# Two transformer blocks on one core: remainder splits, norms and gating rows moved in the order, projection b reads a buffer of its own, down projections start a hidden pair early

## The reference, cut to what matters

```python
# first block
gate_a = sigmoid(...); gate_b = sigmoid(...)
ya = s5_branch(...)                      # [256, 512]
yb = gelu(zu) * (w_s @ layer_norm(gelu(zv)) + bias)   # spatial gating, [256, 1024]
merged = gate_a * (ya @ w_proj_a) + gate_b * (yb @ w_proj_b)
h = h + merged @ w_out
h = h + memory_cross_attention(rms_norm(h, g), memn, ...)
h = h + (silu(hn @ w_gate) * (hn @ w_up)) @ w_down    # F = 2816
# second block, passes c0, x0, c1, x1 (context/tokens of layer 0, 1)
...  merged = sum(gate_i * (y_i @ w_i)) ; h = h + merged @ w_out
...  h = h + (silu(hn @ w1) * (hn @ w3)) @ w2
```

## Time and profile before

| | us |
|---|---|
| median of 3 runs | 2396.34 |
| lowest, highest | 2386.43, 2405.35 |
| the profiled execution, its own time | 2400.58 |
| its span | 2398.1 |
| PE busy | 2208.5 |
| DVE busy | 1619.3 |
| ACT busy | 1006.9 |
| mean granted TensorE clock (share, not us) | 0.964 |

### The profile page before, as it was taken

How to read it: one execution, slowest core, us unless ns; L and a number is a source line. 1 busy time by engine, 2 the same in 40 slices (tenths; PEclk the granted TensorE clock), 3 DMA queues, 4 the chain that set the end, 5 groups by cost and what they waited for, 6 DMA issues and landing times.

```text
span 2398.1 us, 42021 instructions
## 1 busy us (share of the span) xinstructions
PE 2208.5 (92%) x17181; PEld 2064.1 (86%) x17181; DVE 1619.3 (68%) x2081; ACT 1006.9 (42%) x1189; POOL 206.4 (9%) x201
## 2 busy tenths in 40 slices
PE   8898898899999889999999779999999977999998
PEld 6676887799999878899999668899999966889998
DVE  8987554656588876665578967665557896766554
ACT  4114335543444454443444355444344435444332
POOL 3761002100000110000000110000000011000000
PEclk9999999999999999999999889999999988999999
DMA  7678564565555333455555223456545432234552
GB/s 245 245 279 319 208 243 136 177 204 176 188 176 159 123 106 124 158 185 185 179 175 163 88 71 105 142 158 200 186 151 175 141 106 71 89 123 153 180 184 79
DMA packets 290478, 392.99 MB, mean 164 GB/s; under 512 B 8518, under 2 KB 256669, under 8 KB 283677
## 3 DMA queue, kind: packets, MB, share of 16 engines
q1 hardware_dynamic: 285620, 383.53, 49.4%
q10 hardware_dynamic: 3624, 6.31, 0.8%
q0 software_dynamic: 1088, 1.10, 0.2%
HBM read 387.66 MB, written 3.15 MB: 163 GB/s over the span
## 4 chain that ended last, share of the span: by engine, by line
PE 74%; DVE 15%; ACT 4%; issue 3%; DMA 2%; POOL 1%; DVEq 0%; SPq 0%; ACTq 0%
PE L L847 59%; PE M L847 3%; DVE w_rest L430 3%; PE L L1101 2%; PE M L984 2%; PE L L1087 1%; DVE m L1963 1%; DVE n_rest L1972 1%; ACT w_high L424 1%; DMA raw<-in_w_in 1%; PE M L1334 1%; DVE work L2465 1%; DVE work L2593 1%; PE L L1114 1%; DVE rstd L1960 1%
## 5 line engine op out<-in xcount | busy, mean ns | idle before, releaser
L847 PE MATMUL L<-n_high,w_high 128*128 128x256 f32 x3424 | 982.4, 287 | 40.6 <-DVE w_rest L430 20.4
L847 PE MATMUL L<-n_rest,w_high 128*128 128x256 f32 x3424 | 966.2, 282 | 0.0
L847 PE MATMUL L<-n_high,w_rest 128*128 128x256 f32 x3424 | 966.0, 282 | 0.0
L430 DVE TENSOR_TENSOR w_rest<-raw,w_high 128x2048 fp32r<-128x2048 f32 x293 | 671.0, 2292 | 251.3 <-PE L L847 244.0
L424 ACT ACTIVATE w_high<-raw 128x2048 fp32r<-128x2048 f32 x293 | 560.9, 1915 | 398.4 <-PE L L847 364.8
L847 PEld LDWEIGHTS L<-n_high,w_high 128*128 128x128 f32 x3424 | 660.2, 193 | 63.0 <-issue 40.2
L847 PEld LDWEIGHTS L<-n_rest,w_high 128*128 128x128 f32 x3424 | 659.0, 192 | 0.6
L847 PEld LDWEIGHTS L<-n_high,w_rest 128*128 128x128 f32 x3424 | 658.6, 192 | 0.0
L847 PE MATMUL L<-hid_high,w_high 128*128 (+1 forms) x704 | 196.6, 279 | 6.1 <-DVE hid_rest L2390 6.1
L847 PE MATMUL L<-hid_rest,w_high 128*128 (+1 forms) x704 | 195.6, 278 | 0.0
L847 PE MATMUL L<-hid_high,w_rest 128*128 (+1 forms) x704 | 195.5, 278 | 0.0
(11 more groups left out here) (392 smaller groups left out, 2769.7 us busy)
## 6 DMA issues: line engine op xcount, KB each, us to landing
raw<-in_w_in SPq DMA_DIRECT2D x116, 1024.0 KB, 5.5
raw<-in_w_ffn SPq DMA_DIRECT2D x99, 1024.0 KB, 5.3
raw<-in_w_ada SPq DMA_DIRECT2D x32, 1024.0 KB, 6.6
raw<-in_w_out SPq DMA_DIRECT2D x16, 1024.0 KB, 5.0
raw<-in_w_gate SPq DMA_DIRECT2D x11, 1024.0 KB, 5.4
raw<-in_w_up SPq DMA_DIRECT2D x11, 1024.0 KB, 5.3
raw<-in_w_down SPq DMA_DIRECT2D x11, 1024.0 KB, 5.0
work<-in_w_ada SPq DMA_DIRECT2D x8, 1024.0 KB, 7.2
```

Of the source, the lines that this page charges most:

```text
L430: nc.vector.tensor_tensor(w_rest[:, u.first % 2, :], raw[:, u.first % 4, :], w_high[:, u.first % 4, :].bitcast(F32), ALU.subtract).then_in ...
L847: ins = mm(dst, a, b, start=first and i == 0, stop=last and i == 2, skip_group_check=skip)
```

## The change

Seven edits; the first gives a buffer as well, the others move work, waits and releases:

1. yb gets its own place, yb_high in hid_high and yb_rest in the work buffer; proj_b reads it. It is split in gate_b's steps 1 (ACT) and 2 (DVE). The merged rows are split piece by piece beside proj_b's units.
2. The gating rows are called in step 0 of gate_a, behind the split of the weights of gate_a's unit 1. `load_mid(1)` waits for all four gating products.
3. In c0, x0 and x1 the first two pieces of the merged remainder are made between the two proj2 units.
4. A hidden pair's banks are freed behind the product, before the copy and the subtraction.
5. ffn_down starts when all pairs but the last are split, waits for banks 0 and 1, and for banks 2 and 3 after a quarter of its first unit; its last unit waits for the last pair. (proj_a gets the same bank waits.)
6. The norm beside ffn_down moves: squares step 5, sums before unit 6, scaling and remainders four chunks at a time in steps 7 to 9.
7. ffn_down's units are written out on each engine instead of a loop of four.

The functions that only got a range or a buffer as arguments (first_unit, cols_linear, highs_of, rest_chunks, split_high_of, n_split) are left out of the diff:

```diff
--- before.py
+++ after.py
@@ -316,6 +316,8 @@
 
+        yb_high, yb_rest = hid_high[:, 0:DC, :], work_r[:, 2048:4096].rearrange("p (c t) -> p c t", c=DC)
+
         zset = [(m[:, 0:4, :], gate[:, 0:4, :], s5a(4).rearrange(q4, r=4), s5a(5).rearrange(q4, r=4)),
@@ -400,7 +402,7 @@
             first, n = FIRST[name] + start, COUNT[name] - start
-            turns = n // 4
+            turns = 0 if name.endswith("ffn_down") else n // 4
             if turns > 1:
@@ -658,7 +660,7 @@
                 elif i == 1:
-                    sp.wait_ge(sgu_mm, 1)
+                    sp.wait_ge(sgu_mm, 4)
                 else:
...
@@ -928,11 +930,13 @@
 
-            def acc_unit(u, xh, xr, at, first, last):
+            def acc_unit(u, xh, xr, at, first, last, halfway=None):
 
                 wh, wr = parts(u, 2)
                 for c in range(2):
                     for o in range(DC):
+                        if halfway is not None and c == 0 and o == DC // 2:
+                            halfway()
                         ins = product(L[:, o // 2, o % 2 * T:(o % 2 + 1) * T], wh[:, c, o * P:(o + 1) * P],
@@ -943,19 +947,14 @@
                     before[0]()
-                begin(Unit(first), [(b, BANK_USES[name][b]) for b in range(4)])
-                acc_unit(Unit(first), xh, xr, 0, True, n == 1)
-
-                turns = (n - 2) // 4
-                if turns > 1:
-                    with pe.Fori(0, turns) as i:
-                        for k in range(1, 5):
-                            u = Unit(first + k, i)
-                            begin(u, [])
-                            acc_unit(u, xh, xr, 8 * i + 2 * k, False, False)
-                else:
-                    turns = 0
-                for k in range(1 + 4 * turns, n):
+                begin(Unit(first), [(b, BANK_USES[name][b]) for b in range(2)])
+
+                def other_banks():
+                    for b in range(2, 4):
+                        pe.wait_ge(bank_free[b], BANK_USES[name][b])
+                acc_unit(Unit(first), xh, xr, 0, True, n == 1, other_banks)
+
+                for k in range(1, n):
                     if k in before:
@@ -1268,7 +1267,7 @@
             cols_linear("gate_b", before=mid_hooks("gate_b"))
-            cols_linear("proj_b", before=mid_hooks("proj_b"), chunk=split_chunk(0))
+            cols_linear("proj_b", before=mid_hooks("proj_b"), chunk=split_chunk(0), xh=yb_high, xr=yb_rest)
             cols_linear("out", before=mid_hooks("out"), chunk=split_chunk(1))
@@ -1303,8 +1302,11 @@
                     turn_tokens(rows_m, turned)
-                pe.wait_ge(hid_ready, FC // 2 * (HID_OF[pre] + 1))
-                acc_linear(pre + "ffn_down", hid_high, hid_rest, before={9: lambda: norm(next_)} if next_ else {})
+                all_hid = FC // 2 * (HID_OF[pre] + 1)
+                before = {0: lambda: pe.wait_ge(hid_ready, all_hid - 1), FC // 2 - 1: lambda: pe.wait_ge(hid_ready, all_hid)}
+                if next_:
+                    before[6] = lambda: norm(next_)
+                acc_linear(pre + "ffn_down", hid_high, hid_rest, before=before)
 
...
@@ -1726,12 +1728,13 @@
             act.wait_ge(merged, 4)
-            out_to("gate_b", gate, ACT.Sigmoid)
-            multiplied(act, "gate_b")
-            split_high_of(zu, sgu_out, 0)
-            linear("proj_b", None)
-            multiplied(act, "proj_b")
-            split_high_of(m, merged, 4)
+            out_to("gate_b", gate, ACT.Sigmoid, beside={1: lambda: split_high_of(zu, sgu_out, 0, dst=yb_high)})
+
+            def merged_high(b):
+                multiplied(act, "gate_b")
+                split_high_of(m, merged, 4, b0=b, b1=b + 1)
+            linear("proj_b", None, {b + 1: (lambda b=b: merged_high(b)) for b in range(3)})
+            merged_high(3)
             linear("out", None)
@@ -1790,8 +1793,9 @@
 
-                    linear(pre + "ffn_down", None, {8: lambda: squares_of(k, hx if pre == "c0" else hc),
-                                                    9: lambda: (root_of(k), highs_of(k, shift_of[k]))})
+                    linear(pre + "ffn_down", None, {5: lambda: squares_of(k, hx if pre == "c0" else hc), 6: lambda: root_of(k),
+                                                    7: lambda: highs_of(k, shift_of[k], 0, 4),
+                                                    8: lambda: highs_of(k, shift_of[k], 4, DC)})
 
...
@@ -2322,15 +2326,17 @@
             V.tensor_tensor(b_rest[:, :, :], yT, b_high[:, :, :].bitcast(F32), ALU.subtract).then_inc(branch_ready, 1)
-            for b in range(4):
-                dve.wait_ge(sgu_mm, b + 1)
-                x = zu[:, 2 * b:2 * b + 2, :].rearrange("p a t -> p (a t)")
-                for h in range(2):
-                    mixed = M[:, b, h * T:(h + 1) * T].rearrange("p (a t) -> p a t", a=2)
-                    ins = V.tensor_tensor(mixed, mixed, sgu_b[:, 2 * b + h, :].unsqueeze(1).to_broadcast((P, 2, P)), ALU.add)
-                link(ins)
-                V.tensor_tensor(x, x, M[:, b, :], ALU.mult).then_inc(sgu_out, 1)
-            linear("gate_a")
+
+            def gated():
+                for b in range(4):
+                    dve.wait_ge(sgu_mm, b + 1)
+                    x = zu[:, 2 * b:2 * b + 2, :].rearrange("p a t -> p (a t)")
+                    for h in range(2):
+                        mixed = M[:, b, h * T:(h + 1) * T].rearrange("p (a t) -> p a t", a=2)
+                        ins = V.tensor_tensor(mixed, mixed, sgu_b[:, 2 * b + h, :].unsqueeze(1).to_broadcast((P, 2, P)), ALU.add)
+                    link(ins)
+                    V.tensor_tensor(x, x, M[:, b, :], ALU.mult).then_inc(sgu_out, 1)
+            linear("gate_a", beside={0: gated})
             evacuated(dve, "gate_a")
@@ -2346,8 +2352,7 @@
             dve.sem_inc(h_ready, 1)
-            linear("gate_b")
-            n_split(zu, NHIGH_EVENTS["yb"])
+            linear("gate_b", beside={2: lambda: n_split(zu, NHIGH_EVENTS["yb"], to_high=yb_high, to_rest=yb_rest)})
 
@@ -2356,8 +2361,10 @@
                 V.tensor_tensor(mm_, mm_, g, ALU.add).then_inc(merged, 1)
+                if j:
+                    n_split(m[:, :, :], NHIGH_EVENTS["merged"], b0=j - 1, b1=j)
             linear("proj_b", proj_b_out)
-            n_split(m[:, :, :], NHIGH_EVENTS["merged"])
+            n_split(m[:, :, :], NHIGH_EVENTS["merged"], b0=3)
             one = lambda c: flat[:, 1:2]
@@ -2385,12 +2392,11 @@
                     dve.wait_ge(dve_step, done + 1)
+                    dve.sem_inc(bank_free[k2 - 1], 1)
+                    dve.sem_inc(bank_free[k2], 1)
                     V.tensor_copy(hi_, hh).then_inc(dve_step, 1)
                     dve.wait_ge(dve_step, done + 2)
                     V.tensor_tensor(re_, hh, hi_.bitcast(F32), ALU.subtract).then_inc(hid_ready, 1)
-
-                    dve.sem_inc(bank_free[k2 - 1], 1)
-                    dve.sem_inc(bank_free[k2], 1)
 
@@ -2420,8 +2426,10 @@
                     g_, s_ = mix_gain(*p_[1:]), mix_shift(*p_[1:])
-                    linear(name, beside={8: lambda: mean_of(next_),
-                                         9: lambda: (inverse_root(next_), norm_chunks(next_, hc if p_[2] else hx, g_, s_))})
+                    src = hc if p_[2] else hx
+                    linear(name, beside={6: lambda: mean_of(next_), 7: lambda: (inverse_root(next_), scale_chunks(src, g_, 0, 4)),
+                                         8: lambda: (rest_chunks(next_, s_, 0, 4), scale_chunks(src, g_, 4, DC)),
+                                         9: lambda: rest_chunks(next_, s_, 4, DC)})
                 dve.wait_ge(unit_done, FIRST[name] + COUNT[name])
@@ -2614,8 +2622,9 @@
                 unit_ended(p + "proj2", 0)
+                n_split(m[:, :, :], NHIGH_EVENTS[p], 0.5, 0, 2)
                 unit_ended(p + "proj2", 1, more=False)
-                n_split(m[:, :, :], NHIGH_EVENTS[p], 0.5)
+                n_split(m[:, :, :], NHIGH_EVENTS[p], 0.5, 2, 4)
                 add_to_h(p + "out", h, lambda c: mod[:, l, s * 48 + 16 + c:s * 48 + 17 + c])
```

30 lines of the change are left out of this document (15 added, 15 removed).

## The result

The changed kernel takes 2358.09 us (median of 4 runs, 2351.49 to 2362.25). The kernel before took 2396.57 on the same chip (2386.43 to 2405.35), so the ratio is 0.9839, with an interval of 0.9812 to 0.9865: 38.5 us, or 1.6%. A second comparison of the same two kernels gave 2357.85 against 2394.14, ratio 0.9841 (0.9821 to 0.9860). The prediction was 2359, in a range of 2346 to 2378. The mean granted clock rose from 0.964 to 0.971.

The account below looks back on a forecast made before the run. PE's own matmuls and its waits were taken to bound the kernel. Waits 24.3 plus clock 15.0 less pace 1.9 gave 37.4 us, so 2359 from the median of 2396.3, range 2346 to 2378.

Parts of the forecast that it names:

- gating rows, gate_a: In gate_a, unit 1 starts without its 4.59 us wait and unit 2 starts earlier; 4.0 us gained.
- projection b, out: At projection b and stage out, waits of 2.02 and 2.20 us go through earlier splits; 2.0 and 2.2 us gained.
- pass ends, three: At the ends of c0, x0 and x1, waits of 3.52 us shrink by 2.3 each; 6.9 us gained.
- hidden pairs: Before ffn_down, PE needs only the product's end and the bank; 1.16 us each in c0, x0, x1, 3.7 in all.
- ends of ffn_down, three: In first block, c0 and x0, additions into h start when the unit ends; 1.57 us each, 4.7 gained.
- clock: Behind ten waits of over 1.9 us, stretches at granted clock 0.50 go, 1.5 us each; 15.0 us gained.
- pace: In ffn_down, three more units in each of three stages run slower behind the norm's sums; 1.9 us lost.
- Rival (b): The clock comes back only in part: 2374 with none of the ten stretches gone, 2368 with four; chance 0.16.
- Rival (c): The slow pace spreads to two more stages of 1500 matmuls, losing 13 us: 2372; chance 0.10.
- (d): In the first block DMA takes over and the block's gain is lost: 2372.5; chance 0.09.
- (e): Written-out units of ffn_down slow PE's supply of instructions, 2 us a unit: 2423; chance 0.04.
- (f): The change does less than it says, waits moving to the neighbouring engine in most places: 2390; chance 0.03.

Follow-up runs that it names:

- the four parts alone: Kernel before with one part of the change each: first block 2382.9 us, pass ends 2384.2, hidden pairs 2390.86, norm two units earlier 2389.2.
- the nine filled waits: Kernel before plus unread products of the ones matrix (3, 3, 6, 3 or 4 a wait) where PE waited, lengths of waits kept: 2382.27 us against 2392.8.
- the first block alone: Kernel before with only yb's own buffer and split beside gate_b, merged rows split beside proj_b, gating rows in gate_a's step 0: 2382.9 us against 2395.2.
- the written-out run: Kernel before with ffn_down's units written out on all four engines instead of the loop, nothing else: 2392.35 us against 2395.16.
- Two expectations above: Those for the first, larger fillings with products of the ones matrix: kernel before, 2395.05 us (about 2382 expected); changed kernel, 2393.69 (about 2349 expected).

## Why the prediction was right

| step | predicted gain, us | measured in the trace | how |
|---|---|---|---|
| gating rows, gate_a | 4.0 | 3.9 | 4.59 of idle before; 0 at unit 1 and 0.66 at unit 2 now |
| bank wait of proj_a | 0.8 | 0.8 | gone |
| projection b, out | 4.2 | 4.2 | both gone |
| pass ends, three | 6.9 | 6.2 | 3.52 to 1.44 each |
| hidden pairs | 3.7 | 3.0 | 1.97 to 1.04, three times, and 0.2 |
| ends of ffn_down, three | 4.7 | 4.6 | 2.56 to 1.02 each |
| waits together | 24.3 | 22.7 | |
| clock | 15.0 | 16.2 | the first 36 matmuls behind each of the ten waits: 5.6 to 5.8 us before, 4.1 to 4.3 now |
| pace | -1.9 | -1.0 | see below |

The sum of the measured terms is 37.9; the profiled executions differ by 2400.6 - 2358.2 = 42.4, so 4.5 us are in none of them. Of these, 2.5 us are idle time (25.2 less the 22.7 above) in waits that the change does not touch and that differ from one execution to the next, 0.7 lie outside the span, and 1.3 are PE's busy time, which fell by 16.5 where clock and pace make 15.2: half-clock stretches at other places differ too. Over the whole span the mean granted clock gives 18.0 us ((1 - 0.964) x 2398.1 - (1 - 0.971) x 2356.4), which counts all places, and stretches in which PE stood idle. By the medians the gain is 38.5, predicted were 37.4.

**Pass ends.** The mechanism was right, the size 0.2 us each too large. DVE around c0's last unit, as in the earlier trace rows:

```profile
948.41 2.28 DVE L432 TENSOR_TENSOR w_rest<-raw,w_high 128x2048 fp32r<-128x2048 f32 x1
950.61 1.28 DVE L2016 SCALAR_TENSOR_TENSOR n_rest<-m,n_high 128x512 fp32r<-128x512 f32 x2
951.81 0.68 DVE L2031 SCALAR_TENSOR_TENSOR gate<-gate,L 128x512 f32<-128x512 f32 x1
```

PE started again at 952.59 after 1.44 us of idle, so the unit had ended at 951.15. The merge starts 0.66 behind that, where it started 0.04 behind it before (968.59 against 968.55), so it is 0.6 late and not 0.4: its w_rest began 2.74 us before the unit's end, and 2.96 before the end in the earlier trace rows, from which the prediction was worked out. Its first instruction frees the bank at 952.49, and PE starts at 952.59, exactly the chain that the prediction names, with the merge as releaser. The third piece of remainders, called the tightest place, never shows as a wait.

**Hidden pairs.** 0.23 us each too large. The product's end frees the bank only through DVE's own queue:

```profile
1109.41 0.69 DVE L2393 TENSOR_TENSOR gate<-gate,L 128x512 f32<-128x512 f32 x1 [3.29 <-PE L L849]
1110.36 0.43 DVE L2397 CAST hid_high<-gate 128x512 fp32r<-128x512 f32 x1 [0.26 <-DVE gate L2393]
```

DVE stands still 0.26 us behind the product until its own semaphore is seen; the increments that free the banks stand behind that wait, and PE starts at 1110.41, beside the cast. The prediction let PE start at the product's end.

**Ends of ffn_down.** As predicted. The additions into h start as the unit ends, and between 613.9 and 641.9 PE has no wait at all, so DVE's heavy step 7 is covered.

```profile
636.97 2.29 DVE L432 TENSOR_TENSOR w_rest<-raw,w_high 128x2048 fp32r<-128x2048 f32 x1 [1.78 <-PE L L849]
642.55 3.23 DVE L2436 SCALAR_TENSOR_TENSOR hx<-L,flat,hx 128x256 f32<-128x256 f32 x8 [3.29 <-PE L L849]
```

**The clock.** The mechanism is shown, and the size of one stretch was about right: 1.3 to 1.7 us where 1.5 was taken. All ten stretches went, since every wait left there is 1.44 us or less. The number ten was luck.

It belongs to this one execution, and the prediction took it off the median of all. In the traces of this case in which a wait of the kernel before stands unchanged and unfilled, it was followed by 0.50 at gate_a in 7 of 7, at projection b in 3 of 5, at out in 4 of 5, at the pass ends in 13 of 15, at the ends of ffn_down in 14 of 18, and before the later ffn_downs (1.97 us) in 2 of 15. So an average execution of the kernel before has 7.7 such stretches and not ten, and at 1.6 us each they are worth some 12 us (an estimate from these counts) and not 15. The same estimate gives 12, 10, 4 and 6 us for the four parts alone, where the medians gave 12.3, 11.0, 4.3 and 6.0, and 11 for the nine filled waits, where they gave 10.5. For the whole change it gives 34, and the median gain was 38.5 (32 to 45 by the interval). So the clock term was some 3 us too large for an average execution, and that the forecast still came within 1.1 us is luck.

Rival (b), that the clock returns only in part, is out: none of the ten places kept it. The rule of the Trainium skill ("TensorE: Matmul & The Clock Gate", section on oscillation), with waits of 3 to 5 us, would have given 6 us for the four long waits. The traces differ from it: of the nine places with products only three are over 3 us, and the six shorter ones, of 2.0 to 2.6 us, gave 9.6 of the 14.2 us.

**The pace.** Right at its place, with more going on beside it. Windows of L849, PE only: the three stretches behind the norm's sums, then ffn_up of c0 and of x0, and x1's from ffn_up into ffn_down:

```profile
613.90:643.80 29.90, 28.88 (x242) 1.00 0.63 199
1146.40:1176.70 30.30, 29.27 (x245) 1.00 0.62 192
1711.30:1741.60 30.30, 29.28 (x246) 1.00 0.57 174
989.40:1109.20 119.80, 119.06 (x1011) 1.00 0.58 188
1554.00:1674.00 120.00, 119.31 (x1049) 1.00 0.58 188
2164.60:2339.40 174.80, 173.76 (x1534) 1.00 0.51 169
```

Behind the sums it is about 119 ns a matmul in all three, counting restarts (117.8 within a unit), as forecast. But c0's ffn_up now ran at 117.8 ns (113.4 before) and x1's at 113.3 (117.7 before). The two cancel, by chance: slow and fast stages changed places again when the changed kernel was run a second time. Rival (c), that the slow pace spreads, did not come true here. The pace can account for a part of the 10 us by which single runs differ: in the 14 traces, what matmuls of more than 113.4 ns add up to is between 15 and 31 us.

**The other rivals.** (d), DMA takes over in the first block: the first block alone gained 12.3 us, and between 240 and 390 us no wait of PE ends with a load. The prediction said this of the whole block, which is wrong. For one, in the memory attention, behind 390, three waits end with loads of w_ada pieces, 2.6 us together before (0.61, 1.43, 0.56) and 2.5 now. They didn't grow, so the rival is out all the same. (e) fell by the written-out run. (f): each wait went where the prediction had it.

## What to carry to other kernels

An idle stretch of TensorE costs more than its length when it is long enough for the clock to fall behind it: behind waits of 2 to 4.6 us the half clock, where it came, cost 1.3 to 1.7 us on top, and shortening these waits to 1.44 us or less took it away at all ten places. How often it comes behind a wait has to be counted over several executions; one trace is a single draw. So look for work of the neighbouring engine that stands ahead of what TensorE waits for but isn't needed by it, and move it ahead or behind. Waits of 0.7 to 1.6 us of idle time were followed by the half clock in only 9 of 465 cases here. Filling a wait with idle matmuls gives the clock alone, and only where TensorE, and not another engine or a transfer, sets when the next stage ends, where the filler is surely shorter than the wait, and where the clock is not down already.

## What the runs showed of the hardware

**Which waits the clock falls behind.** Over the 14 traces of this case, all gaps between the starts of two matmuls of more than 1 us (from 80 us on; idle time is the gap less 0.28), and how many were followed by a granted clock of 0.50 (the lower level, 1.2 GHz):

| gap, us | gaps | followed by 0.50 |
|---|---|---|
| 1.0 to 1.9 | 465 | 9 |
| 1.9 to 2.1 | 21 | 0 |
| 2.1 to 3.0 | 233 | 163 |
| 3.0 to 3.5 | 42 | 26 |
| over 3.5 | 166 | 164 |

In between, the length of the wait does not decide it: where no edit touched it, the wait of 2.56 us behind ffn_down was followed by it in 14 of 18 cases. What decides was not found. Each gap here is one wait of nearly the same program, so the rows are not independent samples.

**Two paces at a full clock.** Consecutive 128x256 matmuls start 113.4 ns apart in some stages and 117.8 in others, at a granted clock of 1.00 in both, and a stage keeps its pace for a hundred microseconds and more. Of the four runs of 1007 matmuls in a trace (ffn_up, 56 in all) 14 were slow, at no fixed place, 4.4 us longer each; the same kernel had it in c0 in one execution and in the first block and x0 in another. Behind the norm's sums in ffn_down it was the slower in all 42 cases (three in each of 14 traces), to the end of ffn_down at least: some 100 matmuls with the norm before unit 9, some 245 with it before unit 6. What chooses the pace was not found.

**A 32-bit product of the ones matrix** with 128x256 elements shows as two matmul records, 0.43 us at the full clock and 0.85 at half. Two expectations above were wrong for want of this number, though a row with eight such products as sixteen records was there to be read.
